# A streaming encoder layer: conv tails through a small buffer, and three steps of the group loop in another order

## What is computed

```python
xbc, conv_new = causal_dwconv(xbc, conv_ctx, p['ssm_conv_w'], p['ssm_conv_b'])   # 4 taps; conv_new: the last 3 inputs
xbc = silu(xbc);  xs, Bm, Cm = split(xbc)                                        # 8 groups
y, h = ssd_scan(xs * dt, dt * A, Bm, Cm, h0)
...
s = einsum('bcqkrd,bcskd->bckrqs', qc, kb) * HEAD_DIM ** -0.5                    # sliding window, 8 chunks
m = max(max(s), sink);  e = exp(s - m);  pr = e / (sum(e) + exp(sink - m))
o = einsum('bckrqs,bcskd->bcqkrd', pr, vb)
```

## Time and profile before

| | us |
|---|---|
| three runs | 1552.0, 1562.04, 1562.96 |
| their median | 1562.04 |
| the profiled execution | 1553.16 |
| its span | 1551.4 |
| TensorE busy | 1420.6 (92%) |
| VectorE busy | 809.0 (52%) |
| GpSimd busy | 566.9 (37%) |
| ScalarE busy | 489.7 (32%) |

### The profile page before, as it was taken

The page is one execution under the profiler, slowest core; times in us unless marked ns, Lnnn a source line. Parts: engine busy times, 40 slices in busy tenths (PEclk is TensorE's granted clock), DMA queues, the critical chain, the costliest instruction groups (busy, mean ns, idle before and its releaser), DMA issues. The chain is left out here.

```text
span 1551.4 us, 24989 instructions
## 1 busy us (share of the span) xinstructions
PE 1420.6 (92%) x10245; PEld 1265.5 (82%) x10245; DVE 809.0 (52%) x1214; ACT 489.7 (32%) x834; POOL 566.9 (37%) x341
## 2 busy tenths in 40 slices
PE   7899988898988989888889999999899999999994
PEld 1589877787877778777569999995499999999993
DVE  1655239677686875868444200035556666660114
ACT  2323324334252442425343221143223233232221
POOL 0533314243342433425013344332344444443442
PEclk9899979999999999999989999999899999999997
DMA  9274333333343233433455222263032222222221
GB/s 373 105 239 122 111 98 87 95 93 83 110 106 98 86 91 93 107 110 81 151 203 183 79 85 82 95 253 131 4 107 82 83 94 83 84 95 82 82 69 58
DMA packets 87304, 173.57 MB, mean 112 GB/s; under 512 B 37912, under 2 KB 51960, under 8 KB 83760
## 3 DMA queue, kind: packets, MB, share of 16 engines
q1 hardware_dynamic: 87232, 172.53, 35.1%
HBM read 155.20 MB, written 17.76 MB: 111 GB/s over the span
## 5 line engine op out<-in xcount | busy, mean ns | idle before, releaser
L157 POOL TENSOR_TENSOR w_lo<-raw_w,w_hi 128x1024 fp32r<-128x1024 f32 x175 | 428.5, 2449 | 746.1 <-ACT w_hi L151 746.1
L179 PE MATMUL psum<-hp_hi,w_hi 128*128 128x274 f32 x1488 | 460.4, 309 | 30.3 <-ACT raw L878 19.6
L179 PE MATMUL psum<-hp_lo,w_hi 128*128 128x274 f32 x1488 | 441.4, 297 | 0.0
L179 PE MATMUL psum<-hp_hi,w_lo 128*128 128x274 f32 x1488 | 440.8, 296 | 0.0
L151 ACT ACTIVATE w_hi<-raw_w 128x1024 fp32r<-128x1024 f32 x175 | 185.1, 1057 | 621.3 <-PE psum L179 568.5
L179 PEld LDWEIGHTS psum<-hp_hi,w_hi 128*128 128x128 f32 x1488 | 290.9, 196 | 49.3 <-ACT raw L878 21.5
L179 PEld LDWEIGHTS psum<-hp_lo,w_hi 128*128 128x128 f32 x1488 | 293.5, 197 | 0.6
L179 PEld LDWEIGHTS psum<-hp_hi,w_lo 128*128 128x128 f32 x1488 | 291.7, 196 | 0.0
L179 PE MATMUL psum<-hq_hi,w_hi 128*128 128x274 f32 x832 | 244.9, 294 | 7.8 <-POOL hq_lo L1410 4.2
L179 PE MATMUL psum<-hq_hi,w_lo 128*128 128x274 f32 x832 | 244.4, 294 | 0.0
L179 PE MATMUL psum<-hq_lo,w_hi 128*128 128x274 f32 x832 | 243.8, 293 | 0.0
(11 more groups left out here) (226 smaller groups left out, 2071.1 us busy)
## 6 DMA issues: line engine op xcount, KB each, us to landing
raw_w<-in_w_grp SPq DMA_DIRECT2D x57, 512.0 KB, 3.8
raw_w<-in_w_ffn_in SPq DMA_DIRECT2D x44, 512.0 KB, 3.2
ada<-in_w_ada SPq DMA_DIRECT2D x12, 1024.0 KB, 20.2
raw_w<-in_w_ffn_out SPq DMA_DIRECT2D x22, 512.0 KB, 3.3
acs_b<-mem_acs SPq DMA_DIRECT2D x8, 1096.0 KB, 6.7
raw_w<-in_w_ssm SPq DMA_DIRECT2D x16, 512.0 KB, 3.2
ada_o<-in_w_ada SPq DMA_DIRECT2D x4, 2048.0 KB, 10.6
raw_w<-in_w_qkv SPq DMA_DIRECT2D x13, 512.0 KB, 4.8
```

Source lines behind the costliest of these rows:

```text
L157: eng.tensor_tensor(flat(w_lo[self.hl_slot(n)]), raw_w[self.raw_slot(n)][:], flat(w_hi[self.hl_slot(n)]).bitcast(F32), ALU.subtract).then_ ...
L179: mm = pe.matmul(out[:, h, :], w, x[:, cols], start=first and j == 0, stop=last and j == 2)
```

## The change

Three edits. The last three columns of the prompt and of the sample are first copied by GpSimd into a small buffer `tails`; the two stores read that, now in 128 pieces of 12 numbers each, and SyncE waits for the copies ahead of them; `evac(t)` waits for the copies (`tail_s`) and not for the stores. On ScalarE `evac(0)` moves ahead of `split_hi(2)` and the exponentials. On VectorE `at.normalise` moves from behind `conv(2)` to behind `conv(1)`.

```diff
+                tails = sb(st, "tails", [P, 2, 4, TAPS - 1])
...
-                            sp.dma_start(o["conv_p"][bass.ds(g * P, P), :], raw_last(T)).then_inc(cout_s, 16)
-                            sp.dma_start(o["conv_s"][bass.ds(g * P, P), :], raw_last(TW)).then_inc(cout_s, 16)
+                            sp.wait_ge(tail_s, 2)
+                            for n, name in enumerate(("conv_p", "conv_s")):
+                                sp.dma_start(o[name][bass.ds(g * P, P), :], tails[:, n].rearrange("p a b -> p (a b)")).then_inc(cout_s, 16)
...
+                            pool.tensor_copy(tails[:, 0], raw_last(T)).then_inc(tail_s, 1)
+                            pool.tensor_copy(tails[:, 1], raw_last(TW)).then_inc(tail_s, 1)
                             w.split_lo(pool, 1)
                             w.split_lo(pool, 2)
...
                                 if t < 4:
                                     act.wait_ge(conv_s, t + 1)
-                                    act.wait_ge(cout_s, 32)
+                                    act.wait_ge(tail_s, 2)
...
                             w.split_hi(act, 1)
                             tanh(0)
+                            evac(0)
                             w.split_hi(act, 2)
                             at.exps(act)
-                            evac(0)
                             tanh(1)
...
                             conv(1)
+                            at.normalise(dve)
                             silu(0)
                             conv(2)
-                            at.normalise(dve)
                             silu(1)
```

More of the change, by code:

```diff
@@ L776, in build_layer @@
                 h_s0 = sb(st, "h_s0", [P, HPG, HD])
+                tails = sb(st, "tails", [P, 2, 4, TAPS - 1])
                 names = ("g_par g_conv g_th g_silu g_eb g_cdec g_tr g_cb g_xd g_bt g_w g_xt g_dif g_dece g_y g_ds g_ye g_h"
-                         " g_evac g_yout g_out g_acs g_dve g_h0 g_cbe g_conv_out g_ctx")
+                         " g_evac g_yout g_out g_acs g_dve g_h0 g_cbe g_conv_out g_ctx g_tails")
                 handles = sems(st, names)
                 (par_s, conv_s, th_s, silu_s, eb_s, cdec_s, tr_s, cb_s, xd_s, bt_s, w_s, xt_s, dif_s, dece_s, y_s, ds_s,
-                 ye_s, hst_s, evac_s, yout_s, gout_s, acsb_s, dve_s, h0_s, cbe_s, cout_s, ctx_s) = handles
+                 ye_s, hst_s, evac_s, yout_s, gout_s, acsb_s, dve_s, h0_s, cbe_s, cout_s, ctx_s, tail_s) = handles
                 w = Stream(st, "g", [None] * GT, NCH, True, [None] * RAW_SLOTS)
```

## The result

The changed kernel takes 1569.55 us, the median of 8 runs (1566.29 to 1573.92), against 1559.14 for the kernel before on the same chip (8 runs, 1552.0 to 1564.29): a ratio of 1.0076, 95% interval 1.0057 to 1.0096. It is slower, by less than 1%, and the interval leaves out no change, though the prediction held that about 1% is needed for that. Forecast were 1569.0, most likely within 1%, in a range of 1556 to 1580. The profiled execution took 1566.29 us, 13.1 more than that of before.

A forecast was written before the change was run, and what follows sets the result against it. TensorE was taken to set the pace, with delays of the attention's values passed on to the scan. The profiled 1553.2 us plus 15.2 for later values and low clock gave 1568.4, stated as 1569, range 1556 to 1580.

The forecast's parts named there:

- What bounds: In the eight passes TensorE sets the pace, busy 479.5 of 537.5 us; only delays reaching its last matmuls count.
- The wait of 19.6 us: TensorE's seven waits for the evacuation of line 878; the rival that they are simply won gave 1533.6 us, chance 0.05.
- Above 29.5 the delay is passed on in full: Values ending later than about 29.5 us into a pass delay the scan's end by the same amount.
- The other bound, below 29.5: VectorE's silu(3), slowed to 1.29 us behind GpSimd's split, bounds the scan; values ending earlier bring nothing.
- The buffer at 0, the evacuation at nothing seen: GpSimd's two copies cost 0 (at most 0.4 us a pass); evac(0)'s 0.63 us on ScalarE goes unnoticed in group 1.
- tanh(2) pushed by conv(2): On ScalarE, tanh(2) waits for the later conv(2); line 491 starts 22.2 us and values(0) 22.85 us into a pass.
- One long wait: TensorE waits ahead of values(0) for copies of turned probabilities, 5 to 6 us a pass, some 45 us in all.
- The clock term: The low clock behind the long wait lengthens the values by 1.9 us a pass, bounds 0 to 2.8.
- The sum: Over the passes: groups 1 to 6 cost 11.4 us, group 0 3.1, group 7 about 0.7; together 15.2.
- By which way the delay is passed on: On TensorE from the last value product through five filling steps, turn_scores(0), the scan and the last filling steps.
- The rule on the clock: TensorE's default is throttled and activity releases it, so every pass starts its values at the low level after the long idle.

The follow-up runs named there:

- e1: The changed kernel with normalise put back behind conv(2), small buffer and early evac(0) kept; 1549.27 us, ratio 0.9955 to the kernel before.
- e3: The changed kernel with normalise and evac(0) both in their old places, leaving the small buffer alone; 1548.97 us, ratio 0.9972 to the kernel before.
- e2: The kernel before with only normalise moved, ahead of silu(0); 1567.24 us, ratio 1.0084 to the kernel before.
- e6: The changed kernel with tanh(2) moved behind the second pair of copies of turned values; 1550.38 us, ratio 0.997 to the kernel before.
- e4: The changed kernel with 36 products of no use in TensorE's long wait ahead of values(0); 1555.17 us, ratio 0.9993 to the kernel before.
- e5: The changed kernel with three filling steps from behind the values moved into the long wait ahead of values(0); 1563.66 us, ratio 1.0066 to the kernel before.
- e10: e5 with 24 products of no use behind its four filling steps ahead of values(0); 1554.9 us, ratio 0.9984 to the kernel before.
- e9: e4 with 18 products of no use instead of 36; 1564.71 us, ratio 1.0052 to the kernel before.
- e7: e1 with three filling steps moved into its wait for normalise and two moved behind turn_scores(0); 1557.61 us, ratio 1.0017 to the kernel before.
- e8: e7 with GpSimd's split of the fourth tile moved ahead of the decayed C; 1559.88 us, ratio 1.0034 to the kernel before.

## Why the prediction was right, and where it was not

- **What bounds.** Right in effect. The wait of 19.6 us was worth little: in e1, where it is gone and nothing late is put in, the scan ends where it ended in most passes before, and the medians differ by 6.5 us. Above 29.5 the delay is passed on in full, as forecast: in all eight passes of the changed kernel the scan ends 26.5 us behind the values.
- **The other bound, below 29.5.** It is not where I put it. silu(3) ended at 31.4 in group 1 (318.47), and turn_scores(0) came at 32.7, just the five steps behind the values; nothing waited for silu(3). The lead over group 3 is still 0.7 us there, and it is lost at TensorE's next turn but one, which waited 0.62 us for ScalarE's copy of what had been turned before (`bt`, line 886), and ScalarE for VectorE. In group 3 that wait is 0.06. In e1 it comes in all eight passes, 5.1 us in all. The rows of group 1, kernel before:

```profile
325.06 0.63 ACT L884 ACTIVATE dec<-dec 128x512 f32<-128x512 f32 x1 [3.68 <-DVE dec L949]
...
325.95 0.41 PE L1041 MATMUL psum<-ident,cv 128*128 128x128 f32 x2 [0.62 <-ACT bt L886]
```

- **The buffer at 0, the evacuation at nothing seen.** Right for the copies (the split behind them still waits), but e1 and e3 show a gain. That there could be one is the point that I held too low: I had said that values that end earlier bring nothing, and in e1 group 7 and the ends of the passes moved. Measured, the buffer is worth 0.3%, with the early evacuation 0.45%, and the two can't be told apart. Where TensorE then waits instead is for normalise (27.2 us in e1), which I had not named.
- **tanh(2) pushed by conv(2).** Right, to a tenth: 20.2 for tanh(2), 22.2 for line 491, 22.9 for `values(0)` in the passes that start at full clock; e2 shows that moving normalise alone makes the cost, e6 that tanh(2) is the link.
- **One long wait.** Right. Forecast were some 45 us in all and 5 to 6 a pass; measured were 44.8, and 5.4 to 5.8 a pass. (By the prediction's own 304 and 309.95 it would have been 5.95; it wrote 5.5.)
- **The clock term.** I took 1.9 us a pass between bounds of 0 and 2.8. In group 3 it was 8.25 - 6.66 = 1.6, in group 1 the values took 9.55, which is 2.9, and the mean of the eight is 8.71, which is 2.05. What I missed is that the kernel before paid some of it already: in seven of its eight passes a low stretch of 3.4 or 6.8 us lies between 16 and 27 us into the pass, 30.7 us in all (61.4 after), and its values took 7.07 us in the mean. So the change doubled a cost that was there. e4 gives the term as a whole: by the ratios 0.8%, some 1.6 us a pass.
- **The sum.** From the first start to the last, seven passes, the changed kernel takes 15.2 us longer (484.8 against 469.6); I had 14.5 for these. That this is so close is partly luck. The scan ends later by 3.6, 3.1, 3.2, 1.6, 2.5, 2.2 and 2.0 us in these passes, 18.2 in all. Passes 0, 2, 4 and 5 have a low stretch in their first microseconds; there tile 0 is done at 9.7 to 10.8 and not at 8.3, the exponentials end at 14.9 to 16.0, behind conv(1), and everything is 0.7 to 1.8 late. I had that for groups 0 and 7 only. On the other side 3 us come back between the scan and the end of the pass, where the low stretches fall otherwise than before: group 3, whose scan ends 1.6 us later, is only 0.1 us longer as a pass. The rest of the program is 2.1 shorter, 0.4 ahead of the loop and 1.7 in the last pass and behind it. I had counted neither.
- **By which way the delay is passed on.** I wrote that it runs through five filling steps. e5 shows that ScalarE's copy of the result, tanh(3) and silu(3) carry it as well, once fewer steps lie between.
- **The rule on the clock.** In all eight passes of the changed kernel the values start at 1.2 GHz behind waits of 5.4 to 5.8 us; with the wait filled (e4, e10) they run at 2.4 GHz throughout. In group 7 of before, which the prediction likens to this, they started at the high clock and lost it 0.6 us later. The rule that the prediction quotes from the Trainium skill, "TensorE: Matmul & The Clock Gate", section "What's actually happening", that activity releases the throttle, agrees with these rows.

What stays open: why the runs of one and the same kernel spread over some 12 us. The time goes with the granted clock: of 68 runs of the kernel before in the experiments, the 17 with a mean clock of 0.947 to 0.952 took 1555.8 to 1565.6 us, the 16 with 0.956 to 0.959 took 1548.1 to 1554.8. So the slower runs hold more low stretches. Where these lie, and why they differ, isn't shown, since only one execution of each kernel was profiled. For the same reason the rows of one pass are an example, and the ratios are the measure.

## What to carry to other kernels

A wait that the table names longest may be worth nothing: look, in passes that differ by chance, at whether the end of the stage follows it. When a step is moved up on one engine, ask what is moved down by it and whose instruction waits for that at the head of another engine's list: here 2.3 us of normalise moved conv(2), conv(2) held tanh(2), and tanh(2) held copies that had long been ready to go. In this kernel a long wait of TensorE was paid twice, since the work behind it ran at the low clock (8.71 us in the mean and not 6.67), and it had to be filled nearly to its end before much came back. And compare an experiment with the kernel that shares its other edits: beside the kernel before, the gain of the small buffer hid about a third of what the early normalise costs.

## What had not been expected of the hardware

- Filling 2.3 of 5.5 us of a wait (e9) left the values at 8.2 us, filling 4.6 (e4) brought them to 6.67.
- Moving work forward on the bounding engine cost time: in e7 turn_scores(0) comes 1.3 us sooner and the scan ends about 1.2 later.
- The small stores landed in 7.7 and 9.8 us as 512 pieces of 12 bytes and in 5.7 and 5.8 as 128 pieces of 48 bytes (from issue to landing, group 1 of before and group 3 of after). Over the eight passes it was 6.7 to 10.5 and 9.8 to 11.4 before, 5.5 to 5.8 and 5.7 to 6.3 after:

```profile
out_conv_p<-raw SPq DMA_DIRECT2D x1, 6.0 KB, 7.7
out_conv_s<-raw SPq DMA_DIRECT2D x1, 6.0 KB, 9.8
```

```profile
out_conv_p<-tails SPq DMA_DIRECT2D x1, 6.0 KB, 5.7
out_conv_s<-tails SPq DMA_DIRECT2D x1, 6.0 KB, 5.8
```
- VectorE was slow beside GpSimd's split: its eight multiplications of normalise took 4.04 us in e8, where the split ran beside them, and 1.93 in e7, where it did not.
